# Attention with V stationary and normalised probabilities, head pairs on two array halves, maxima per four heads: a hybrid attention and MoE layer on one core

## The reference, cut to what matters

```python
def rms_norm(x, g):
    xf = x.astype(jnp.float32)
    y = xf * lax.rsqrt(jnp.mean(xf * xf, axis=-1, keepdims=True) + RMS_EPS)
    return (y * g.astype(jnp.float32)).astype(x.dtype)
...
# group B, one block of 128 queries (group A: the same with bias, 3 patterns merged by lse)
sc = jnp.einsum('bqhd,bkhd->bhqk', qblk, k).astype(jnp.float32) * scale
sc = jnp.where(kpos[None, :] <= qpos[:, None], sc, -jnp.inf)
p = jax.nn.softmax(sc, axis=-1)
return jnp.einsum('bhqk,bkhd->bqhd', p.astype(v.dtype), v)
...
# after attention: both groups concatenated, one output projection, residual,
# RMS norm, router with top 4 of 32 experts, clamped SwiGLU experts
logits = (h @ router_w).astype(jnp.float32) + router_b.astype(jnp.float32)
top_val, top_idx = lax.top_k(logits, TOP_K)
gates = jax.nn.softmax(top_val, axis=-1)
...
glu = gate * jax.nn.sigmoid(SWIGLU_ALPHA * gate)
return ((up + 1.0) * glu) @ w_down[e] + b_down[e]
```

## Time and profile before

| | us |
|---|---|
| median of 3 runs | 1077.78 (1077.39 to 1078.17) |
| the profiled execution's own time | 1077.39 |
| its span in the trace | 1075.6 |
| TensorE busy | 997.1 (93%) |
| DMA | 423.50 MB, 394 GB/s over the span |
| chain that ended last | TensorE 52%, DMA 46% |
| output projection's first part begins in that chain | 117.64 |
| expert loop begins | 156.26 |

### The profile page before, as it was taken

How to read it: one execution, slowest core, us unless ns; L and a number is a source line. 1 busy time by engine, 2 the same in 40 slices (tenths; PEclk the granted TensorE clock), 3 DMA queues, 4 the chain that set the end, 5 groups by cost and what they waited for, 6 DMA issues and landing times.

```text
span 1075.6 us, 12397 instructions
## 1 busy us (share of the span) xinstructions
PE 997.1 (93%) x4752; PEld 410.3 (38%) x4752; DVE 205.0 (19%) x443; ACT 131.4 (12%) x262; POOL 62.0 (6%) x138
## 2 busy tenths in 40 slices
PE   7999999999999999998898988888888898988888
PEld 4546653434343434343333333333333233323333
DVE  1046233111111111111111111111111111101112
ACT  2235221000000000000000000000000000000000
POOL 0250000000000000000000000000000000000000
PEclk9999999999999999999999999999999999999999
DMA  9669749999999999999999999999999999999995
GB/s 311 191 167 373 314 166 381 429 427 392 379 432 428 428 429 428 428 429 428 428 428 429 429 428 429 428 429 428 429 428 428 428 428 428 429 428 428 429 428 220
DMA packets 40746, 423.50 MB, mean 394 GB/s; under 512 B 6214, under 2 KB 8412, under 8 KB 16156
## 3 DMA queue, kind: packets, MB, share of 16 engines
q1 hardware_dynamic: 38920, 422.85, 94.8%
q10 hardware_dynamic: 1812, 0.46, 0.2%
HBM read 420.68 MB, written 2.62 MB: 394 GB/s over the span
## 4 chain that ended last, share of the span: by engine, by line
PE 52%; DMA 46%; ACT 1%; issue 1%; SPq 0%; DVE 0%; ACTq 0%
DMA dring<-in_w_down_dram 45%; PE bank L706 17%; PE bank L763 15%; PE bank L508 6%; PE bank L664 3%; PE bank L625 3%; PE bank L686 2%; PE bank L696 1%; PE bank L549 1%; PE bank L516 1%; DMA ring<-in_w_in_dram 1%; ACT mt L911 1%; PE bank L753 1%; PE bank L611 0%; PE bank L576 0%
## 5 line engine op out<-in xcount | busy, mean ns | idle before, releaser
L706 PE MATMUL bank<-ring,mt 128*64 128x512 f32 x2048 | 452.5, 594 | 0.1
L763 PE MATMUL bank<-dring,mt 128*64 128x512 f32 x1024 | 231.1, 597 | 65.7 <-DMA dring<-in_w_down_dram 55.3
L706 PEld LDWEIGHTS bank<-ring,mt 128*64 128x64 f32 x2048 | 144.8, 137 | 297.0 <-issue 285.4
L1171 DVE TENSOR_SCALAR mt<-bank 128x512 f32<-128x512 f32 x32 | 22.1, 692 | 729.5 <-PE bank L706 729.5
L763 PEld LDWEIGHTS bank<-dring,mt 128*64 128x64 f32 x1024 | 69.7, 136 | 206.6 <-issue 127.4
L909 ACT ACTIVATE mt<-mt 128x512 f32<-128x512 f32 x32 | 20.1, 630 | 450.4 <-DVE mt L1171 450.4
L917 ACT ACTIVATE short<-bank 64x512 f32<-64x512 f32 x64 | 37.9, 592 | 274.0 <-PE bank L763 273.7
L664 PEld LDWEIGHTS bank<-mt,hn 128*128 128x128 f32 x544 | 62.2, 192 | 13.8 <-issue 13.0
L664 PE MATMUL bank<-mt,hn 128*128 128x128 f32 x544 | 65.7, 278 | 0.7 <-DVE mt L1074 0.7
L686 PE MATMUL bank<-short,mt 128*128 128x512 f32 x136 | 62.9, 605 | 1.3 <-ACT short L917 1.3
L508 PE MATMUL bank<-ring,mt 128*128 128x512 f32 x128 | 58.5, 612 | 1.4 <-DMA ring<-in_w_in_dram 1.4
(11 more groups left out here) (169 smaller groups left out, 364.4 us busy)
## 6 DMA issues: line engine op xcount, KB each, us to landing
ring<-in_w_gate_up_dram SPq DMA_DIRECT2D x128, 2048.0 KB, 30.6
dring<-in_w_down_dram SPq DMA_DIRECT2D x64, 2048.0 KB, 25.4
ring<-in_w_in_dram SPq DMA_DIRECT2D x4, 1024.0 KB, 11.9
ring<-in_w_in_dram SPq DMA_DIRECT2D x2, 2048.0 KB, 20.8
dring<-in_w_out_dram SPq DMA_DIRECT2D x2, 2048.0 KB, 25.4
dram_bias<-ring SPq DMA_DIRECT2D x1, 1536.0 KB
xs<-in_x_dram SPq DMA_DIRECT2D x2, 512.0 KB, 4.8
mt<-in_w_kv_b_dram SPq DMA_DIRECT2D x1, 1024.0 KB, 12.8
```

The lines of the kernel that those rows point to most:

```text
L706: last = nc.tensor.matmul(ps[64 * h:64 * h + 64, :], xeT[:, k, b * SLOT:(b + 1) * SLOT], GU[b][:, k, u * FF + h * HALF:u * FF + (h + 1) * ...
L763: last = nc.tensor.matmul(ps_a[64 * h:64 * h + 64, :], hT[:, o:o + SLOT], DN[:, c * 4 + k, h * HALF:(h + 1) * HALF], start=c == 0 and k == ...
```

## The change

1. **Rotary parts turned two heads at once.** trq and trk transpose two 128 x 128 blocks in place of four 128 x 64 ones; head g lies on rows 64 (g mod 2).
2. **Score heads in pairs.** Even and odd heads alternate, in two banks, on the two row halves of the array. In group B two plain parts are followed by the two rotary parts, one on each half. Tile 0's group B takes two banks in place of one.
3. **Maxima per four heads.** DVE masks four heads, takes their maximum (`max{t}{m}`), and goes on; exponentials wait for the maximum of their four heads. The reciprocals are one of twelve heads (tile 0) and three of four heads (tile 1), written into DVE's order.
4. **Normalised before the transpose.** The exponentials are multiplied by the reciprocal denominators in SBUF: five multiplications of 128 x 512 on GpSimd (n00, n01, n02, n10, n11), four on DVE (n12 to n15). The transposes P0g and P1g wait for these.
5. **V stationary.** The values are computed with V as the stationary operand and 128 columns of transposed probabilities as the moving one, so that features lie on partitions; group A's heads alternate between the two column halves. The results are copied to `mixT` (vA by ACT, vB by DVE), and the sixteen transposes mT and their four copies are gone.
6. **Order on ACT:** exponentials of tile 0, of heads 0 to 7 of tile 1, copies P00 to P02, exponentials of heads 8 to 11 of tile 1, pV1, vA0, P10, P12, P14, vA1.
7. `mixT` and `h2T` change places in SBUF, the first fills of `GU[1]` wait for `max12` where they waited for `max1`, and the banks of gate, up and output accumulators follow the new length of the job list.

```diff
-        qTr = tcut(4 * SEQ)[0:ROPE].rearrange("p (h t) -> p h t", h=4)
+        qTr = tcut(4 * SEQ)[:, 0:2 * SEQ].rearrange("p (h t) -> p h t", h=2)
...
-                turn(f"trq{t}", [sq[:, 1024 + t * 512:1024 + t * 512 + 256].rearrange("p (h r) -> p h r", h=4)[:, h, :] for h in range(4)], ROPE)
+                turn(f"trq{t}", [sq[:, 1024 + t * 512 + j * P:1024 + t * 512 + (j + 1) * P] for j in range(2)])
...
-            for name, (t, heads) in heads_of.items():
-                b = begin(name)
+            def scores(t, even, odd):
                 nk = (t + 1) * P
+                banks = {even: begin(even), odd: begin(odd)}
...
+                for pair in zip(*(heads_of[n][1] for n in (even, odd))):
+                    outs = [banks[place_of[t, h][0]][:, place_of[t, h][1] * nk:(place_of[t, h][1] + 1) * nk] for h in pair]
+                    if pair[0] < A_HEADS:
+                        for n, h, o in zip((even, odd), pair, outs):
+                            r = slice(64 * (h % 2), 64 * (h % 2) + 64)
+                            last[n] = nc.tensor.matmul(o, qTa[r, h // 2, t * P:(t + 1) * P], kTa[r, h // 2, 0:nk], start=True, stop=True)
                     else:
+                        for h, o in zip(pair, outs):
+                            nc.tensor.matmul(o, qTn[:, h - A_HEADS, t * P:(t + 1) * P], kTn[:, h - A_HEADS, 0:nk], start=True, stop=False)
+                        for n, h, o in zip((even, odd), pair, outs):
+                            g = h - A_HEADS
+                            r = slice(64 * (g % 2), 64 * (g % 2) + 64)
+                            last[n] = nc.tensor.matmul(o, qTr[r, g // 2, t * P:(t + 1) * P], kTr[r, g // 2, 0:nk], start=False, stop=True)
...
             for g in range(3):
-                pe.wait_ge(act_steps, ACTS.at(f"e0{4 * g + 3}"))
+                pe.wait_ge(pool_steps, POOL.at(f"n0{g}"))
                 turn(f"P0{g}", [prob[0][:, 4 * g + j, :] for j in range(4)])
...
+            b = begin("vA1")
+            for j in range(4):
+                if j % 2:
+                    pe.wait_ge(dve_steps, DVE.at(f"P1{j}"))
+                else:
+                    pe.wait_ge(act_steps, ACTS.at(f"P1{j}"))
+                for kt in range(2):
+                    for h in (2 * j, 2 * j + 1):
+                        last = nc.tensor.matmul(b[64 * (h % 2):64 * (h % 2) + 64, j * P:(j + 1) * P], value(h, kt), turned(h, kt),
+                                                start=kt == 0, stop=kt == 1)
+            PE.done("vA1", last)
...
-            for t in range(TT):
-                pe.wait_ge(dve_steps, DVE.at(f"vB{t}"))
-                for g in range(2):
-                    turn(f"mT{t}{g}", [mixed[:, t, (4 * g + j) * P:(4 * g + j + 1) * P] for j in range(4)])
...
-                pe.wait_ge(act_steps, ACTS.at(f"mT{t}1"))
+                pe.wait_ge(act_steps, ACTS.at(f"vA{t}"))
+                pe.wait_ge(dve_steps, DVE.at(f"vB{t}"))
...
+            exponentials(0, range(12))
+            exponentials(1, range(8))
+            for g in range(3):
+                copied(f"P0{g}", probT0[:, g * 512:(g + 1) * 512], bank[job_at[f"P0{g}"] % 8][:, :])
+            exponentials(1, range(8, 12))
             scaled("pV1", pr[:, 1, 1024:1536], 512, r_x[:, 1:2])
+            copied("vA0", mixT[:, 0:4, 0:P], of("vA0"))
             for g in range(0, 6, 2):
                 copied(f"P1{g}", probT1[g], bank[job_at[f"P1{g}"] % 8][:, :])
+            copied("vA1", mixT[:, 0:4, P:SEQ], of("vA1"))
...
+            for m in range(3):
+                masked(0, m)
+            masked(1, 0)
+            reciprocals("rden0", 0, 0, 12)
+            masked(1, 1)
+            reciprocals("rden10", 1, 0, 4)
+            masked(1, 2)
+            reciprocals("rden11", 1, 4, 4)
+            own("rden11")
+            weighted(2)
+            weighted(3)
+            mixed(0)
+            reciprocals("rden12", 1, 8, 4)
+            own("rden12")
+            weighted(4)
+            weighted(5)
             for g in range(1, 6, 2):
-                copied(f"P1{g}", probT1[g])
+                DVE.done(f"P1{g}", V.tensor_copy(probT1[g], ps(f"P1{g}")))
+            mixed(1)
...
+            for g in range(3):
+                weighted(f"n0{g}", prob[0][:, 4 * g:4 * g + 4, :], den[:, 0, 4 * g:4 * g + 4], [P, 4, P], "rden0")
+            for g in range(2):
+                weighted(f"n1{g}", prob[1][:, 2 * g:2 * g + 2, :], den[:, 1, 2 * g:2 * g + 2], [P, 2, SEQ], "rden10")
```

More of the change, by code:

```diff
@@ L320, in layer_kernel @@
                      + [f"{n}{t}" for t in range(2) for n in ("tnk", "trq", "trk", "tak")]
-                     + [f"e{t}{h}" for t in range(2) for h in range(12)] + ["pV1"]
-                     + [f"P1{g}" for g in range(0, 6, 2)]
-                     + [f"mT{t}{g}" for t in range(2) for g in range(2)]
+                     + [f"e0{h}" for h in range(12)] + [f"e1{h}" for h in range(8)] + ["P00", "P01", "P02"]
+                     + [f"e1{h}" for h in range(8, 12)] + ["pV1", "vA0", "P10", "P12", "P14", "vA1"]
                      + ["sq2_00", "sq2_01", "hn0", "sq2_10", "exp0", "sq2_11", "hn1", "exp1"])
@@ L328, in layer_kernel @@
                     + [f"{n}{t}" for t in range(2) for n in ("tnq", "taq")]
-                    + [x for n, (t, hs) in heads_of.items() if t == 0 for x in [f"{n}{h}" for h in hs]] + ["max0"]
-                    + [x for n, (t, hs) in heads_of.items() if t == 1 for x in [f"{n}{h}" for h in hs]] + ["max1"]
-                    + ["rden0", "P00", "P01", "P02", "vA0", "vB0", "rden1", "P11", "P13", "P15", "vA1", "vB1"]
+                    + [f"s0h{h}" for h in range(0, 4)] + ["max00"] + [f"s0h{h}" for h in range(4, 8)] + ["max01"]
+                    + [f"s0h{h}" for h in range(8, 12)] + ["max02"]
+                    + [f"s1h{h}" for h in range(0, 4)] + ["max10", "rden0"] + [f"s1h{h}" for h in range(4, 8)] + ["max11", "rden10"]
+                    + [f"s1h{h}" for h in range(8, 12)] + ["max12", "rden11", "n12", "n13", "vB0", "rden12", "n14", "n15"]
+                    + ["P11", "P13", "P15", "vB1"]
                     + ["low", "low4", "first0"]
@@ L417, in _ @@
                 if g == 0:
-                    sp.wait_ge(dve_steps, DVE.at("max1"))
+                    sp.wait_ge(dve_steps, DVE.at("max12"))
                 if g == 2:
@@ L580, in value @@
+            for t, even, odd in ((0, "s0e", "s0o"), (0, "s0x", "s0y"), (1, "s1a", "s1b"), (1, "s1c", "s1d"), (1, "s1e", "s1f")):
+                scores(t, even, odd)
             def value(h, key_tile):
@@ L587, in _ @@
             for g in range(3):
-                pe.wait_ge(act_steps, ACTS.at(f"e0{4 * g + 3}"))
+                pe.wait_ge(pool_steps, POOL.at(f"n0{g}"))
                 turn(f"P0{g}", [prob[0][:, 4 * g + j, :] for j in range(4)])
[L590 to L596, removed]
+            b = begin("vA0")
@@ new lines, in _ @@
+            for h in range(8):
+                pe.wait_ge(act_steps, ACTS.at(f"P0{h // 4}"))
+                last = nc.tensor.matmul(b[64 * (h % 2):64 * (h % 2) + 64, (h // 2) * P:(h // 2 + 1) * P], value(h, 0),
+                                        probT0[:, h * P:(h + 1) * P], start=True, stop=True)
+            PE.done("vA0", last)
+            b = begin("vB0")
+            pe.wait_ge(act_steps, ACTS.at("P02"))
+            for h in range(8, 12):
+                last = nc.tensor.matmul(b[:, (h - 8) * P:(h - 7) * P], value(h, 0), probT0[:, h * P:(h + 1) * P], start=True, stop=True)
@@ L598, in _ @@
+            PE.done("vB0", last)
             for g in range(6):
-                pe.wait_ge(act_steps, ACTS.at(f"e1{2 * g + 1}"))
+                if g < 2:
+                    pe.wait_ge(pool_steps, POOL.at(f"n1{g}"))
+                else:
+                    pe.wait_ge(dve_steps, DVE.at(f"n1{g}"))
                 turn(f"P1{g}", [prob[1][:, 2 * g + j // 2, (j % 2) * P:(j % 2 + 1) * P] for j in range(4)])
[L601 to L612, removed]
@@ L617, in out_project @@
+            PE.done("vA1", last)
+            b = begin("vB1")
+            pe.wait_ge(act_steps, ACTS.at("P14"))
+            pe.wait_ge(dve_steps, DVE.at("P15"))
+            for h in range(8, 12):
+                for kt in range(2):
+                    last = nc.tensor.matmul(b[:, (h - 8) * P:(h - 7) * P], value(h, kt), turned(h, kt), start=kt == 0, stop=kt == 1)
+            PE.done("vB1", last)
             def out_project(t, g):
                 pe.wait_ge(ld[f"wout{g}"], 16)
-                pe.wait_ge(act_steps, ACTS.at(f"mT{t}1"))
+                pe.wait_ge(act_steps, ACTS.at(f"vA{t}"))
+                pe.wait_ge(dve_steps, DVE.at(f"vB{t}"))
@@ L999, in _, with masked @@
             dve.wait_ge(ld["const"], 16)
-            for t in range(TT):
+            def masked(t, m):
                 nk = (t + 1) * P
[L1002 to L1011, removed]
@@ L1022, in _ @@
[L1022 to L1029 removed]
+                for h in range(4 * m, 4 * m + 4):
+                    n, j = place_of[t, h]
```

(3 more changed lines are left out.)

99 lines of the change are left out of this document (44 added, 55 removed).

## The result

The changed kernel takes 1070.67 us (median of 4 runs, 1069.96 to 1071.18) where the kernel before takes 1077.97 us beside it: 7.3 us less, ratio 0.9933 with a 95% interval of 0.9921 to 0.9944. The profiled execution took 1069.96 us, its span is 1068.2 us. The forecast was 1072.2 us, with a range from 1070.3 to 1075.5.

A forecast was written before the change was run, and what follows sets the result against it. TensorE bounds the kernel to 482 us, then the down-weight load, whose last hole TensorE ends. Savings of 3.25 before pV1's end, 1.88 (mT), 1.5 (values), less 0.8 (modes) and 0.5 (waits), give X 5.5: 1072.2 us, range 1070.3 to 1075.5.

The forecast's parts named there:

- The rival by which DMA takes up the gain: DMA-bound second half: attention's gain fills a hole and is lost, 1077.8 us; chance of gain lost or not made 0.10.
- stretched by GpSimd: DVE work from 94.65 to 100.8 us takes 1.75 times as long: X 2.8, 1075.0 us; chance 0.13.
- the slower case: GpSimd's 128 x 512 multiplications, forecast 1.3 us each, take 3.9 us and delay the output projection: 1080.8 us; chance 0.05.
- X: How much earlier than 117.64 us the output projection's first piece, oP00, starts: forecast 5.5 us.
- pairing gives 0: Group A's scores: records already paced by weight loads in tile 0, heads already overlapping in tile 1; gain taken as 0.
- tile 0's rotary pairs at 0.43 us: Group B scores, tile 0: two rotary matmuls run at the pace of their four weight loads, 0.43 us a pair.
- Values at 0.08 us a record: Group A's values, loading 64 weight columns: the middle between 0.056 and 0.111 us a record.
- From pV1 to P12: After pV1 ends at 100.3 us: P0 turns, ACT copies at 0.60 us each, last exponentials, pV1 scaled by 105.4 us.
- The wait ahead of P12: P12 needs the bank of pV1, which ACT frees at 105.4 us: a new TensorE wait of 0.4 us.
- Changes of mode at 0.2 us each: TensorE's scores and values: each change of operand height or tiling mode costs 0.2 us; group A's values add four, 0.8 us.
- four heads and their maximum: DVE masking four heads and taking their maximum: 1.89 us for tile 0, 2.96 us for tile 1.
- 1.9 us of slack on the last maximum: Tile 1's last maximum, forecast at 100.8 us, may be 1.9 us late before ACT, waiting for TensorE's P02, notices.

The follow-up runs named there:

- the delay: Changed kernel with P15's four transposes made eight times (28 more, 3.05 us of TensorE work) ahead of tile 1's values: 1072.44 us.
- the late fills: Changed kernel with the last two fills of the second gate and up buffer waiting for oP01 instead of vB1: 1069.95 us.
- the two later ones: The changed kernel again, unchanged, compared with the kernel before on two different chips: 1070.13 and 1069.63 us.
- The serial experiment: Changed kernel with group A's score heads in the old order, all even heads and then all odd heads: 1071.66 us.
- values serial: Changed kernel with group A's value matmuls on one column half after the other, even heads then odd, in both tiles: 1072.54 us.
- the kernel with both edits: Changed kernel with pV1 scaled by DVE instead of ACT and group B's rotary score parts ahead of the plain ones: 1067.99 us.

## Why the prediction was right, and where it was short

The mechanism by which time saved reaches the end held; what failed, on the safe side, are terms of the sum. TensorE ends the last hole in the weight stream, behind it lies a fixed 782.5 to 782.9 us in all thirteen profiles, and a shift of the output projection reaches the end one to one. The rival by which DMA takes up the gain is refuted by the delay (3.05 us in, 3.05 us out by its profile, the clock apart) and by the stages of all the others; the late fills show that the gain did not come from earlier loads. DVE was not stretched by GpSimd, and GpSimd's multiplications took 1.01 us each, not 1.3, so the slower case was never near.

The size was short. X, as the prediction defines it, is 117.64 - 110.10 = 7.54 us, where the forecast was 5.5; counted from the first transpose it is 7.76, 2.3 more than the forecast. In the medians it is 7.3 us, forecast 5.6. The prediction's range ended at X = 7.5, so the profile lies just outside it, the first comparison (1070.67 us, the range began at 1070.3) just inside, and the two later ones, 8.0 and 7.9 us faster, outside again. That the time fell into the range was in part luck, since the four misjudged terms below all err to the same side and nothing makes up for them. By terms:

| term | forecast | measured | difference |
|---|---|---|---|
| turns | 4.5 | 4.54 | 0 |
| group A scores, both tiles | 3.48 | 1.09 + 1.73 | -0.66 |
| group B scores, tile 0 | 2.52 | 2.12 | -0.40 |
| group B scores, tile 1 | 3.38 | 3.38 | 0 |
| end of pV1 to start of P12 | 5.25 | 4.72 | -0.53 |
| P12 to output projection | 6.55 | 5.81 | -0.74 |

1. *Group A, "pairing gives 0".* This step failed. I read 0.103 us a record as the pace of weight loads that come one after another; it is the pace at which one half of the array takes streams of 128 columns, and the other half can work beside it. The single records of tile 0 in the trace show it: in the changed kernel an even and an odd head's record start 0.007 us apart, and each half starts its next one 0.111 us later, so 16 records are eight steps and a tail. In the kernel before a half starts one every 0.111 us too, but the halves work together only where the two groups of eight meet. That it is the stream and not the load shows in the step on one half: 0.111 us with 128 loaded and 128 streamed columns, 0.216 us with 128 loaded and 256 streamed (tile 1), 0.109 us with only 64 loaded and 128 streamed (the values). The row I took the pace from the earlier trace rows has about the same 0.112 us for 128 loaded columns with 64 or 128 streamed, so it couldn't tell the two apart. The serial experiment put the 0.65 us back. The same mistake priced tile 0's rotary pairs at 0.43 us in place of 0.22 (0.42 with the change of height).
2. *Values at 0.08 us a record.* The middle was the wrong choice: 0.054 us (1.73 us of weight loads for 32 records), the lower end. The Trainium skill, TensorE: Matmul & The Clock Gate, section LDWEIGHTS, gives about 53 ns to load 64 columns. The trace has the same number, but not for that reason: with the same loads on one half the records start every 0.109 us, and 0.054 is that step shared by two halves. On the scores its rule of about 107 ns for 128 columns does not bound the pace either, since both halves take such loads side by side.
3. *From pV1 to P12.* ACT's copies start 0.52 us apart, not 0.60 (three in 1.57 us); I used the duration of one where the spacing counts, which is 0.24 of the 0.53 us. The four exponentials took 1.95 us where I had 2.06, pV1 0.59 where I had 0.68, and the first copy came 0.48 us behind pV1's end where I had 0.6. The wait ahead of P12 was forecast at 0.4 us and is 0.42.
4. *Changes of mode at 0.2 us each* held: tile 1's group B is at 3.38 us as computed, and grouping the rotary parts, which takes six such changes away, saved 1.18 us. The rule of the Trainium skill, TensorEngine Tiling (Array Packing), section Key Properties, that such a change drains TensorE, fits this; the trace shows the cost, not the drain itself.

One more sum was wrong and cost nothing: four heads and their maximum stand at 1.89 and 2.96 us in the prediction, while its own figures from the earlier trace rows add up to 1.76 and 2.82, and 1.76 and 2.8 us are what the timeline shows. So the last maximum came at 99.3 us, not 100.8; it was not on the chain.

The prediction had 1.9 us of slack on the last maximum and named TensorE as the owner of the path. The chain after shows ACT there for 4.1 us, which that sum had in its numbers (copies, exponentials, pV1, then P12) but the text called only a wait of 0.4 us. Taking the maxima per four heads back costs 2.50 us, and pairs and rotary parts alone bring 3.45 of the 7.76 us. The parts lean on each other, so these worths need not add up. No run takes back the V stationary form or the normalisation on GpSimd alone; what they brought is read from pieces only (tile 1's values 5.36 us before and 3.88 after, the sixteen transposes of 1.88 us gone).

## What to carry to other kernels

When a stream of loads bounds the second half of a kernel, look for the last hole in it and for who ends it: work ahead of that point counts in full, and loads ahead of the hole may start later without cost (14 us for two of them here). Order matmuls that use half of the array so that neighbours use different halves, and group them by operand height; the matmuls stay the same ones. When TensorE's work shrinks, follow the freed time into the engine that empties its banks, and price that engine by the spacing of its instructions, not by the duration of one.

## What the runs showed of the hardware

**The clock falls in the router stage of some executions.** In three of thirteen profiles (values serial, delay, both) the sixteen gather records ahead of the experts take 3.6 to 3.7 us where the others have 2.05. The stretches of the kernel with both edits, and then the same gather in the changed kernel (the third number from the right is the granted clock):

```profile
140.00:142.00 2.00, 1.82 (x17) 1.71 (x16) 1.10 (x7) 1.75 (x1) 0.16 (x1) 1.00 1.01 426
142.00:144.00 2.00, 1.26 (x7) 1.15 (x8) 0.61 (x3) 0.62 (x2) 0.00 (x0) 0.78 0.94 401
144.00:146.00 2.00, 2.00 (x11) 2.00 (x11) 0.69 (x1) 0.00 (x0) 0.00 (x0) 0.50 0.00 0
146.00:148.00 2.00, 2.00 (x12) 0.93 (x12) 0.69 (x1) 0.00 (x0) 0.00 (x0) 0.87 0.00 0
```

```profile
146.00:148.00 2.00, 1.41 (x12) 1.41 (x13) 0.64 (x4) 0.23 (x2) 0.00 (x0) 1.00 0.71 303
```

Granted 0.50 is 1.2 of 2.4 GHz. Ahead of it TensorE had waited for DVE twice, 0.18 and 0.74 us, while it did short matmuls of the router; the changed kernel has the same two waits and keeps 1.00. What decides between the two is not shown. It costs 1.45 us: 173.8 in place of 172.3 us in the table above.

**Matmuls on half of the array run beside those on the other half, loads included.** On one row half a float32 record of 128 streamed columns starts every 0.111 us, and with even and odd heads alternating both halves keep that step, 0.007 us apart. In the mean of a piece, with its ends, it is 0.068 us a record when alternating and 0.103 when not. The listed duration of a load is 187 ns in both (137 ns for the values' loads, in both orders too): it says little about the pace.
